# Six raw tiles and nine split halves, quads 0 and 1 made ahead, and another order of the first quad's products, in a two-block forward pass on one core

## What is computed

```python
h2 = rmsnorm(x, norm2_g[l])
x = x + jnp.square(jax.nn.relu(h2 @ w_mlp_in[l])) @ w_mlp_out[l]
```

## Time and profile before

| what | us |
|---|---|
| median of 3 runs | 2805.14 (2802.98 to 2805.68) |
| profiled execution | 2803.97 |
| its span | 2802.2 |
| PE busy | 2783.2 |
| VectorE (DVE) busy | 2229.2 |
| ScalarE (ACT) busy | 1578.9 |

### The profile page before, as it was taken

One profiled execution on the slowest core, in us unless ns is written; L12 is line 12 of the kernel. 1 busy time (PEld: TensorE's weight loads), 2 busy tenths in 40 slices (PEclk: granted clock), 3 DMA queues, 4 the chain that ended last, 5 costly groups with the idle time before them and its releaser, 6 DMA issues.

```text
span 2802.2 us, 34047 instructions
## 1 busy us (share of the span) xinstructions
PE 2783.2 (99%) x13066; PEld 2294.5 (82%) x13066; DVE 2229.2 (80%) x2506; ACT 1578.9 (56%) x1796; POOL 2.6 (0%) x7
## 2 busy tenths in 40 slices
PE   9999999999999999999999999999999999999998
PEld 7888878888887888888888888888888888888887
DVE  6698855656778999999967678877678999999985
ACT  6644445544455666666656444444455666666664
POOL 0000000000000000000000000000000000000000
PEclk9999999999999999999999999999999999999999
DMA  9576646656876677766677666667676766676774
GB/s 329 157 226 203 204 151 213 199 192 202 265 214 223 210 248 246 238 218 235 219 251 218 225 199 217 200 206 223 206 235 202 250 219 233 218 248 233 248 234 148
DMA packets 372643, 617.01 MB, mean 220 GB/s; under 512 B 23041, under 2 KB 96385, under 8 KB 371841
## 3 DMA queue, kind: packets, MB, share of 16 engines
q1 hardware_dynamic: 372048, 614.51, 67.6%
q10 hardware_dynamic: 432, 0.32, 0.0%
HBM read 577.26 MB, written 2.10 MB: 207 GB/s over the span
## 4 chain that ended last, share of the span: by engine, by line
PE 89%; DVE 7%; issue 1%; ACT 1%; DMA 1%; ACTq 0%; DVEq 0%
PE ACC L927 76%; PE TB L934 7%; PE ACC L934 5%; DVE WLS L1704 1%; DVE FG L1719 1%; DVE TSL L1730 1%; DVE FG L1721 1%; DVE FG L1723 1%; DVE YBL L1730 1%; DVE YAL L1730 1%; DMA RAW<-in_w_up_dram 1%; ACT X L1549 0%; DMA RAW<-in_w_mlp_in_dram 0%; PE TB L1054 0%; DVE XTL L2272 0%
## 5 line engine op out<-in xcount | busy, mean ns | idle before, releaser
L1704 DVE TENSOR_TENSOR WLS<-RAW,WHS 128x1024 fp32r<-128x1024 f32 (+1 forms) x1023 | 1174.8, 1166 | 406.2 <-ACT WHS L1205 404.8
L1205 ACT ACTIVATE WHS<-RAW 128x1024 fp32r<-128x1024 f32 (+1 forms) x1023 | 1009.3, 1012 | 702.5 <-PE ACC L927 573.9
L927 PE MATMUL ACC<-WHS,XTH 128*128 128x512 f32 (+1 forms) x1692 | 658.3, 389 | 0.0
L927 PE MATMUL ACC<-WLS,XTH 128*128 128x512 f32 (+1 forms) x1692 | 655.4, 387 | 0.0
L927 PE MATMUL ACC<-WHS,XTL 128*128 128x512 f32 (+1 forms) x1692 | 655.3, 387 | 0.0
L927 PEld LDWEIGHTS ACC<-WHS,XTH 128*128 128x128 f32 x1692 | 317.9, 188 | 65.5 <-issue 0.4
L927 PEld LDWEIGHTS ACC<-WHS,XTL 128*128 128x128 f32 x1692 | 317.8, 188 | 64.8
L927 PEld LDWEIGHTS ACC<-WLS,XTH 128*128 128x128 f32 x1692 | 317.9, 188 | 64.0
L927 PE MATMUL ACC<-WHS,YAH 128*128 128x512 f32 x864 | 336.4, 389 | 0.0
L927 PE MATMUL ACC<-WLS,YAH 128*128 128x512 f32 x864 | 336.3, 389 | 0.0
L927 PE MATMUL ACC<-WHS,YAL 128*128 128x512 f32 x864 | 336.3, 389 | 0.0
(11 more groups left out here) (397 smaller groups left out, 3347.3 us busy)
## 6 DMA issues: line engine op xcount, KB each, us to landing
RAW<-in_w_in_dram SPq DMA_DIRECT2D x255, 512.0 KB, 4.5
RAW<-in_w_mlp_out_dram SPq DMA_DIRECT2D x128, 512.0 KB, 5.8
RAW<-in_w_down_dram SPq DMA_DIRECT2D x128, 512.0 KB, 5.6
RAW<-in_w_mlp_in_dram SPq DMA_DIRECT2D x115, 512.0 KB, 4.5
RAW<-in_w_up_dram SPq DMA_DIRECT2D x115, 512.0 KB, 4.6
RAW<-in_w_gate_dram SPq DMA_DIRECT2D x96, 512.0 KB, 4.3
YT<-HT SPq DMA_DIRECT2D x208, 128.0 KB, 3.2
RAW<-in_w_branch_dram SPq DMA_DIRECT2D x48, 512.0 KB, 4.1
```

The source lines that it names most:

```text
L927: ins = e.matmul(ACC[:, 2 * (b % 2) + half, 0:n], p[:, k, xs], q[:, t, 0:n], start=(k == 0 and m == 0 and b not in SEEDED), stop=(k == nk ...
L1205: e.activation(halves(WHS, u)[:, :, 0:n], RAW[u % NRAW][:, ts, 0:n], ACT.Copy).then_inc(hi, 1)
L1704: e.tensor_tensor(l, r, h, ALU.subtract).then_inc(lo, 1)
```

## The change

It sets `NRAW` to 6 and the ring to nine half tiles (a raw tile and a half of `WHS` with `WLS` both take 4 KB of a partition), has quads 0, 2, 4 and 6 in the first pairs, makes quads 0 and 1 ahead with another order of the buffers, and in each pair's first quad has PE take the seven products in another order. There T4's product comes first in the odd unit. In the first pairs the even unit waits for the first of the three steps of the low input sums only, and the odd unit for the second and third where they are used.

```diff
-NRAW = 5
-NSPL = 5
+NRAW = 6
+NHALF = 9
...
-    FIRST_I = (0, 2, 3, 5)
-    MADE_AHEAD = (0, 3)
-    SETS = ("T", "Y", "T", "H", "Y", "T", "H")
+    FIRST_I = (0, 2, 4, 6)
+    MADE_AHEAD = (0, 1)
+    SETS = ("T", "H", "Y", "T", "H", "Y", "T")
...
-    NH = 2 * NSPL
+    NH = NHALF
...
-    WHS, WLS = sb("WHS", [P, 2 * NSPL, 512], F32R), sb("WLS", [P, 2 * NSPL, 512], F32R)
+    WHS, WLS = sb("WHS", [P, NHALF, 512], F32R), sb("WLS", [P, NHALF, 512], F32R)
...
             if m == 0:
                 if rec.first:
-                    e.wait_ge(xs_lo, 3 * (n // 7 + 1))
+                    e.wait_ge(xs_lo, 3 * (n // 7) + 1)
                     e.wait_ge(acc[b0 % 2], b0 // 2)
                 three(acc_bank(b0, 0), sums(S_A), w[0], rec.first, rec.last)
                 three(TB[0][:, :], x(2 * i + 1, 0), w[1], i == 0, False).then_inc(mm, 1)
                 return
+            if rec.first:
+                e.wait_ge(t_lo, 2 * rec.q + 2)
+                three(TB[2][:, :], x(2 * i + 1, 1), weight_sums(T4), True, False)
+                e.wait_ge(xs_lo, 3 * (n // 7) + 2)
+                three(acc_bank(b0, 1), sums(S_2), weight_sums(T2), True, False)
+                e.wait_ge(xs_lo, 3 * (n // 7) + 3)
+                three(TB[1][:, :], sums(S_4), w[1], True, False)
+                e.wait_ge(acc[(b0 + 1) % 2], (b0 + 1) // 2)
+                three(acc_bank(b0 + 1, 0), sums(S_1), weight_sums(T1), True, False)
+                three(acc_bank(b0 + 1, 1), sums(S_3), weight_sums(T3), True, False).then_inc(mm, 1)
+                return
             three(TB[1][:, :], sums(S_4), w[1], i == 0, False)
             e.wait_ge(t_lo, 2 * rec.q + 1)
             three(acc_bank(b0, 1), sums(S_2), weight_sums(T2), rec.first, rec.last)
-            if rec.first:
-                e.wait_ge(acc[(b0 + 1) % 2], (b0 + 1) // 2)
             three(acc_bank(b0 + 1, 0), sums(S_1), weight_sums(T1), rec.first, rec.last)
```

## The result

The changed kernel takes 2818.68 us (median of 4 runs, 2818.47 to 2819.30) against 2804.06 of the kernel before on the same chip (4 runs): a ratio of 1.0053, 95% interval 1.0039 to 1.0067. It is slower by 14.6 us, half a per cent, where +7.8 was forecast. The profiled execution took 2818.67 us, its span 2816.9; PE is busy for 2782.0 us of it, 1.2 less than before, so all of the loss is PE's waiting.

The account below looks back on a forecast made before the run. PE was taken as the bound, busy 2783.2 of 2802.2 us, so only its idle time could change. Eleven pairs +11.2, the twelfth +0.1, the two first pairs -3.5 sum to +7.8 on 2803.97: 2812 us, range 2792 to 2820.

Parts of the forecast that it names:

- What bounds it: Whole kernel: PE is busy 2783.2 of 2802.2 us and no matmul goes, so only PE's idle time can change.
- Quad 1 ahead: Start of each pair: ScalarE copies X out earlier, so PE's wait at the second block's bank goes, 0.6 us a pair.
- The walk: VectorE's and ScalarE's work followed through a pair: the seventh quad starts 1.02 us later, +11.2 us in eleven pairs.
- the twelfth: Twelfth pair: VectorE was already 0.9 us late behind a raw tile's load, which six tiles should cover, so only +0.1 us.
- The gap before h+3: VectorE, before cutting the weights of the third unit after a pair's first unit h: 1.0 us idle, waiting for ScalarE's cut.
- The two first pairs: First two pairs: shorter waits for the input sums and before quad 4, 1.6 to 2 us each, -3.5 us together.
- Everywhere else the later gate costs nothing: Outside the pairs: cuts waiting one unit (2.72 us) longer cost nothing, needing about 2.3 us and getting 8.16.
- The last rival: Second layer: nine halves delay cuts beside VectorE's transposes and residuals, 0.8 us a stage, 11 in all, 2823 us; chance 0.10.
- VectorE arrives in time: Rival, in the pairs: without VectorE's two idle gaps (1.8 us) both PE stalls go, -16.4 us, 2788 us; chance 0.20.
- break-even: Rival, in the pairs: shorter VectorE quads or smaller gaps keep pairs even, first pairs' 3.5 us remain, 2797 to 2806; chance 0.20.

Follow-up runs that it names:

- the first run: The changed kernel with the old rings put back (5 raw tiles, 10 halves), all else as changed: 2811.47 us, 1.0027 of the kernel before.
- the run with both: The changed kernel with the old rings (5 raw tiles, 10 halves) and ScalarE's copy of X one unit later: 2800.44 us, 0.9989 of the kernel before.

## Why the prediction was right or wrong

**What bounds it** was right: only PE's waiting changed, and the time went up, as forecast.

**Quad 1 ahead**: the wait for the copy of X went as said. The 0.6 us a pair are won at that point only. With quads 0 and 3 ahead and the new product order it went too, and all of it came back before the seventh quad.

**The walk**: +1.02 us a pair was forecast, and 0.95 came in eleven pairs and nearly nothing in the twelfth, as said; 10.5 us against 11.3. Each station of it came within 0.1 us, counted from the pair's start. Two of its reasons were less good than its numbers. The gap before h+3 was 0.17 and not 1.0, its rest being spread over the cuts before. And I named that gap as a cause: with ten halves it makes no difference, since h+4 behind the copy sets quad 3's sums alone. That the pair depends on the start of quad 2's sums, 1.2 us of the kernel for each 0.1, was therefore wrong for the changed kernel: the first run moved that start by 0.6 us and the stage did not move. It matters only once the queue of copy and h+4 is out of the way, as in the run with both. The low parts of quad 2 are the point to watch.

**The two first pairs**: -3.5 forecast, -3.6 measured (1.64 and 1.92), split as said between the input sums and quad 4, with 0.7 to 1.0 of it to be had from a sixth raw tile as well.

**"Everywhere else the later gate costs nothing"** is the step that failed. It cost 6.8 us, as much as the whole distance between +7.8 and +14.6. The sentence asked whether a cut still ends before its use. It does, in all units outside the pairs. But both engines work in order, and what stands behind a gated cut is held as well: in the blocks of two and three units a merge that frees a bank, at the output projection the low parts of its input. The last rival had the right mechanism, halves that bite where VectorE has other work, at 0.8 us a piece, but in the wrong place: in the second layer with its four-unit blocks nothing was lost. The rule of the Trainium skill that was named with it ("Perfetto Trace Analysis", section Optimization Strategy, that the same gap repeating can mean too few buffers) is borne out in these short blocks: with ten halves the gap of 0.89 us and its like are gone, though with nine halves and the merges earlier most of them are gone too. In the pairs it would have misled; there the same wait of 1.6 us (19.5 / 12) repeats with nine halves and with ten.

**"VectorE arrives in time" and "break-even"** did not come. Nearest to the first came ten halves and the copy one unit later together, and even there a stage is 83.07 and not the 82.3 that its matmuls need. The figure of the Trainium skill for VectorE's instructions ("VectorE: DVE Perf Modes", section on the TRN2 errata), 6.29 us a quad by the prediction's working, is not borne out: a quad takes 6.72 us after as before. A part of the difference shows in the rows: from one sum to the next, which needs its result, it is 1.25 us (1116.22 to 1117.47), and between two instructions of that size that do not need each other 1.14 (1785.67 to 1786.81). The prediction's working with the figure has a slip besides, on which nothing else rests: 1.7 us off +1.02 puts the pair 0.7 us ahead and not 0.4.

**The number**: 2812 was forecast and 2818.68 came. It lies above the forecast's own range (2806 to 2817) and only 1.3 us inside the whole one (2792 to 2820), whose upper part was there for the last rival. That it is inside is in part luck: 6.8 us that the forecast put at nothing. In the profiled executions the terms differ from the forecast by -0.8 (twelve pairs), -0.1 (first pairs), +6.8 (gate), -0.2 (rest) and +1.2 at the start of the kernel, which is no part of the change, as the last section shows.

## What to carry to other kernels

When a change makes an engine wait for something later, ask of each place not only whether that instruction is still in time but what stands behind it in the same queue and who waits for that; short blocks with an eviction in them are the first to look at. When a stall is taken away in front of an engine that lives on its lead over another, walk on to the next point where the two meet: the 0.6 us won at the bank were due again 26 us later. And test such a walk by moving one instruction at a time: where a fixed set of instructions must pass through one queue, putting one ahead of another only changes which of them is late.

## What the runs showed of the hardware

The start of the kernel is not steady. The sixth unit ended at 26.1 us in the profile before, at 27.25 in the changed kernel, and over the ten profiles anywhere from 26.08 to 27.6, with five and with six raw tiles alike (27.23 with five, 26.08 with six). In most of them the first matmuls show where it comes from; in the profile after:

```profile
7.49 0.63 PE L916 MATMUL ACC<-WLS,XTH 128*128 128x512 f32 x1
7.92 0.63 PE L916 MATMUL ACC<-WHS,XTL 128*128 128x512 f32 x1
```

They follow each other by 0.43 us, and so do those after them up to 10.1 us; in the profile before it is 0.23 from 7.35 on. 512 columns in 0.43 us are 1.19 a nanosecond, which fits the lower of TensorE's two clock levels (1.2 GHz). That is read from the distance of starts alone: the granted clock of the profile shows 1.00 for both stretches. What PE did before was the same in both, ten rows of zero matmuls (`zeros`, the last at 5.25) and then a wait of 1.0 to 1.2 us. In five of the ten profiles the first matmuls come 0.43 us apart, and the sixth unit ended at 26.9 to 27.4; in four they come 0.23 apart, and it ended at 26.1 to 26.4. In the tenth, with quads 0 and 3 ahead again, they come 0.23 apart too, and yet it has the latest end, 27.6, as PE waited another 1.4 us for its weights at 10.1. So 1 us between two single profiles of this kernel says nothing about the change. What kept the clock down in some executions was not looked into; in one of the five (old rings and the copy later) it was up for the first two distances and then down.
